# Key latent first, and the memory output weights in two strips, in a three-block transformer kernel

## The reference, cut to what matters

```
x = x + 0.5 * swiglu(rms_norm(x, ffn1_norm), ffn1_w_in, ffn1_w_out)
z = rms_norm(x, mix_norm) @ w_mix_in
z_mla, z_swa, z_na = split(z)                 # cq (256) | ckv (128) | rotary key (32) = z_mla
  q  = rms_norm(cq, g)  @ w_uq                # 8 heads of 96
  kv = rms_norm(ckv, g) @ w_ukv               # 8 heads of 64 (key) + 64 (value)
x = x + concat(norm(mla), norm(swa), norm(na)) @ w_mix_out
x = x + mem_xattn(rms_norm(x, g), mem, ...)   # o (512 x 256) @ w_o (256 x 1024)
x = x + 0.5 * swiglu(rms_norm(x, ffn2_norm), ffn2_w_in, ffn2_w_out)
x = rms_norm(x, block_norm)
```

## Time and profile before

| | |
|---|---|
| time, median of 3 runs | 3268.42 us (3264.87 to 3268.74) |
| time of the profiled execution | 3268.41 us |
| its span, first to last instruction | 3266.6 us |
| PE busy | 3000.9 us, 92% of the span |
| DVE, ACT, POOL busy | 1460.0, 1086.3, 251.1 us (45%, 33%, 8%) |
| mean granted PE clock | 0.960 of full |
| the 16 DMA engines, busy | 21.4% for the main queue's packets |

### The profile page before, as it was taken

How to read it: one execution, slowest core, us unless ns; L and a number is a source line. 1 busy time by engine, 2 the same in 40 slices (tenths; PEclk the granted TensorE clock), 3 DMA queues, 4 the chain that set the end, 5 groups by cost and what they waited for, 6 DMA issues and landing times. The chain is left out here.

```text
span 3266.6 us, 37293 instructions
## 1 busy us (share of the span) xinstructions
PE 3000.9 (92%) x13472; PEld 2357.7 (72%) x13472; DVE 1460.0 (45%) x2022; ACT 1086.3 (33%) x1770; POOL 251.1 (8%) x184
## 2 busy tenths in 40 slices
PE   8878998999799998998889999699998998899997
PEld 5567676678588887577668888488885677668885
DVE  5653255643444423555344442444424554354432
ACT  4412233343233312555242321232213654333221
POOL 0000000000200012000220002200021001120011
PEclk9989899999899999999999999799998999999998
DMA  3100220113223323010212232132322110122231
GB/s 121 45 20 7 75 77 33 58 46 96 97 96 96 101 96 109 16 56 20 70 60 96 96 102 78 60 96 97 105 83 91 33 52 27 45 91 96 96 104 69
DMA packets 69081, 238.07 MB, mean 73 GB/s; under 512 B 10353, under 2 KB 14449, under 8 KB 68209
## 3 DMA queue, kind: packets, MB, share of 16 engines
q1 hardware_dynamic: 66960, 227.87, 21.4%
q10 hardware_dynamic: 2016, 8.84, 0.7%
HBM read 234.58 MB, written 2.10 MB: 72 GB/s over the span
## 5 line engine op out<-in xcount | busy, mean ns | idle before, releaser
L368 PE MATMUL bank<-L_h_hi,L_w_hi 128*128 128x512 f32 x1808 | 720.9, 399 | 72.3 <-DVE L_h_lo L477 39.0
L369 PE MATMUL bank<-L_h_lo,L_w_hi 128*128 128x512 f32 x1808 | 712.9, 394 | 0.0
L370 PE MATMUL bank<-L_h_hi,L_weight_ring_low 128*128 128x512 f32 x1808 | 712.9, 394 | 0.0
L356 ACT CAST L_w_hi<-L_weight_ring 128x1024 fp32r<-128x1024 f32 (+2 forms) x292 | 326.3, 1118 | 952.0 <-PE bank L370 946.7
L362 DVE TENSOR_TENSOR L_weight_ring_low<-L_weight_ring,L_w_hi 128x1024 fp32r<-128x1024 f32 (+2 forms) x292 | 401.4, 1375 | 358.9 <-ACT L_w_hi L356 358.9
L368 PEld LDWEIGHTS bank<-L_h_hi,L_w_hi 128*128 128x128 f32 x1808 | 345.2, 191 | 162.0 <-issue 56.8
L370 PEld LDWEIGHTS bank<-L_h_hi,L_weight_ring_low 128*128 128x128 f32 x1808 | 344.9, 191 | 72.8
L369 PEld LDWEIGHTS bank<-L_h_lo,L_w_hi 128*128 128x128 f32 x1808 | 345.4, 191 | 71.6 <-issue 1.0
L368 PE MATMUL bank<-L_act_hi,L_w_hi 128*128 128x512 f32 x704 | 273.9, 389 | 0.0
L369 PE MATMUL bank<-L_act_lo,L_w_hi 128*128 128x512 f32 x704 | 273.9, 389 | 0.0
L370 PE MATMUL bank<-L_act_hi,L_weight_ring_low 128*128 128x512 f32 x704 | 273.9, 389 | 0.0
(11 more groups left out here) (283 smaller groups left out, 3878.9 us busy)
## 6 DMA issues: line engine op xcount, KB each, us to landing
L_weight_ring<-ffn_in SPq DMA_DIRECT2D x176, 512.0 KB, 3.4
L_weight_ring<-ffn_out SPq DMA_DIRECT2D x64, 704.0 KB, 4.1
B_weight_ring<-w_sqk SPq DMA_DIRECT2D x24, 512.0 KB, 3.4
B_weight_ring<-w_dn SPq DMA_DIRECT2D x16, 512.0 KB, 3.5
B_weight_ring<-w_gate SPq DMA_DIRECT2D x16, 512.0 KB, 3.4
L_weight_ring<-w_sna_qk SPq DMA_DIRECT2D x16, 512.0 KB, 3.4
L_weight_ring<-w_mix_out SPq DMA_DIRECT2D x16, 512.0 KB, 3.5
B_weight_ring<-w_sv SPq DMA_DIRECT2D x12, 512.0 KB, 3.5
```

The lines of the kernel that those rows point to most:

```text
L356: e.copy(hv.high(at)[:, 0:width], sh.ring[:, at % RING, 0:width]).then_inc(hv.w_hi_done, 1)
L368: e.matmul(out, a_hi, b_hi, start=start, stop=False)
L369: e.matmul(out, a_hi, b_lo, start=False, stop=False)
L370: return e.matmul(out, a_lo, b_hi, start=False, stop=stop)
```

## The change

It has two parts.

**Latents.** The three latent strips are loaded in the order ckv, cq, cq, so that ckv lies in bank 4 and cq in banks 5 and 6. The sum of ckv's squares (into bank 0) moves ahead of the last strip, krope; the two for cq stay behind it (bank 1). ACT makes ckv's 1/rms before it squares the rotary key, and DVE writes the normalised ckv before it touches the rotary key. PE then makes v_mla after waiting only for ckv (lat_done 1), in banks 0, 2, 3 and 4, and waits for the other latents behind v_mla. As bank 0 is also the first job's, that job gets a wait for ACT's first copy of v_mla.

**Memory output.** The host lays w_mem_o out as two strips of 128 x 1024, each for four tiles of x. PE runs the eight tiles in straight code, signalling mem_mm after the tiles that do not end a strip. Since six strips fewer pass the ring, the next block's first two strips lie in it before the memory attention ends. ACT splits the first ahead of its copies of the transposed result and the second behind them; DVE splits both ahead of its first addition to x.

```diff
             mix_jobs.append(dict(parts=[[(0, cq[:, 0, :]), (P, cq[:, 1, :])]], rows=(0, P), width=T,
                                  ones=(ones, QK2), scale=1.0 / QK2, gain=qg[:, 0:1], rope="own", cos_sin=cs2,
-                                 dest=(qk[:, tile, :], QK2), split=h == MLA_HEADS - 1))
+                                 dest=(qk[:, tile, :], QK2), split=h == MLA_HEADS - 1,
+                                 **({"needs": (v_done, TT + 1)} if h == 0 else {})))
...
-                for i in range(3):
+                for i in (2, 0, 1):
                     at = load_strip(e, seen, sh, at, A["w_latent"][layer, i])
...
-                at = resid_sp(e, seen, sh, at, lambda n, part: A["w_mem_o"][layer, n], 1)
+                for i in range(2):
+                    at = load_strip(e, seen, sh, at, A["w_mem_o"][layer, i])
...
+                def lat_sum(k):
+                    e.wait_ge(sh.squared, seen.ready(sh.squared))
+                    e.matmul(banks[0 if k < 1 else 1][:, :], ones, sh.sq[:, k % 2, :], start=(k != 2),
+                             stop=(k != 1)).then_inc(sh.sum_mm, 1)
...
-                e.wait_ge(v_done, seen.ready(v_done, TT))
-                for k in range(3):
-                    e.wait_ge(sh.squared, seen.ready(sh.squared))
-                    e.matmul(banks[0 if k < 2 else 1][:, :], ones, sh.sq[:, k % 2, :], start=(k != 1),
-                             stop=(k != 0)).then_inc(sh.sum_mm, 1)
-                e.wait_ge(lat_done, seen.ready(lat_done, 4))
+                    if i == 2:
+                        e.wait_ge(v_done, seen.ready(v_done, TT))
+                        lat_sum(0)
+                lat_sum(1)
+                lat_sum(2)
+                e.wait_ge(lat_done, 1)
                 w = strip_here(e, seen, sh, at)
                 at += 1
                 for t in range(TT):
-                    mm = e.matmul(banks[4 + t][:, :], ckv[:, 0, t * P:(t + 1) * P], w[:, 0:512], start=True,
+                    mm = e.matmul(banks[(0, 2, 3, 4)[t]][:, :], ckv[:, 0, t * P:(t + 1) * P], w[:, 0:512], start=True,
                                   stop=True)
                 mm.then_inc(sh.strip_done, 1)
                 seen.ready(v_done, TT)
+                e.wait_ge(lat_done, seen.ready(lat_done, 4))
...
-                at = resid_pe(e, seen, sh, at, o_memT, 1, 2)
+                for n in range(KT):
+                    e.wait_ge(sh.x_done, seen.free(sh.x_done))
+                    if n % 4 == 0:
+                        w = strip_here(e, seen, sh, at)
+                        at += 1
+                    for k in range(2):
+                        c = (n % 4 * 2 + k) * P
+                        mm = e.matmul(banks[4 + n % 2][:, :], w[:, c:c + P], o_memT[:, k, :], start=(k == 0),
+                                      stop=(k == 1))
+                    mm.then_inc(sh.strip_done if n % 4 == 3 else mem_mm, 1)
```

More of the change, by code:

```diff
@@ L1398, in _, with latent_rstd @@
                     e.copy(grid_tiles(v_rows[1 + f]), grid_rows(banks[1 + f][:, :])).then_inc(vt_done, 1)
+                def latent_rstd(n, bank, dst):
+                    e.wait_ge(sh.sum_mm, seen.ready(sh.sum_mm, n))
+                    e.activation(dst[:, :], banks[bank][:, :], ACT.Ln, scale=1.0 / (n * P),
+                                 bias=EPS).then_inc(sh.ln_done, 1)
+                    e.wait_ge(sh.ln_done, seen.ready(sh.ln_done))
+                    e.activation(dst[:, :], dst[:, :], ACT.Exp, scale=-0.5).then_inc(sh.rstd_done, 1)
                 for k in range(3):
@@ L1408, in _ @@
                             e.copy(v_sna[:, t, :], banks[t][:, 0:384]).then_inc(v_done, 1)
+                latent_rstd(1, 0, lat_rstd)
                 e.wait_ge(sh.strip_done, seen.ready(sh.strip_done))
                 e.activation(jb.sq[NOPE:QK2, 1, :], banks[7][NOPE:QK2, :], ACT.Square).then_inc(kr_sq, 1)
-                for i, (n, bank, dst) in enumerate(((2, 0, sh.rstd), (1, 1, lat_rstd))):
-                    e.wait_ge(sh.sum_mm, seen.ready(sh.sum_mm, n))
-                    e.activation(dst[:, :], banks[bank][:, :], ACT.Ln, scale=1.0 / (n * P),
-                                 bias=EPS).then_inc(sh.ln_done, 1)
-                    e.wait_ge(sh.ln_done, seen.ready(sh.ln_done))
-                    e.activation(dst[:, :], dst[:, :], ACT.Exp, scale=-0.5).then_inc(sh.rstd_done, 1)
+                latent_rstd(2, 1, sh.rstd)
                 e.wait_ge(sh.strip_done, seen.ready(sh.strip_done))
                 for t in range(TT):
-                    e.copy(v_mla[:, t, :], banks[4 + t][:, :]).then_inc(v_done, 1)
+                    e.copy(v_mla[:, t, :], banks[(0, 2, 3, 4)[t]][:, :]).then_inc(v_done, 1)
                 def group_norms():
@@ L1513, in _ @@
                 seen.ready(sh.strip_done, 9)
+                e.wait_ge(sh.rstd_done, seen.ready(sh.rstd_done))
+                e.scalar_tensor_tensor(out=ckv[:, 0, :],
+                                       in0=banks[4][:, :], scalar=g("ckv"), in1=lat_rstd[:, :],
+                                       op0=ALU.mult, op1=ALU.mult).then_inc(lat_done, 1)
                 e.wait_ge(kr_sq, 1)
@@ L1526, in _ @@
                 for k in range(2):
-                    e.scalar_tensor_tensor(out=cq[:, k, :], in0=banks[4 + k][:, :], scalar=g("cq")[:, k:k + 1],
+                    e.scalar_tensor_tensor(out=cq[:, k, :], in0=banks[5 + k][:, :], scalar=g("cq")[:, k:k + 1],
                                            in1=sh.rstd[:, :], op0=ALU.mult, op1=ALU.mult).then_inc(lat_done, 1)
-                e.wait_ge(sh.rstd_done, seen.ready(sh.rstd_done))
-                e.scalar_tensor_tensor(out=ckv[:, 0, :],
-                                       in0=banks[6][:, :], scalar=g("ckv"), in1=lat_rstd[:, :],
-                                       op0=ALU.mult, op1=ALU.mult).then_inc(lat_done, 1)
                 def scale_groups():
@@ L1586, in _ @@
                            unit=attn_dve_steps(e, seen, sh, at_, mem_units, stores("mem", o_mem, 2)))
+                for i in range(2):
+                    split_strip_dve(e, seen, sh, hv, ffn2_at + i, W_IN)
                 for n in range(KT):
-                    e.wait_ge(sh.strip_done, seen.ready(sh.strip_done))
+                    if n % 4 == 3:
+                        e.wait_ge(sh.strip_done, seen.ready(sh.strip_done))
+                    else:
+                        e.wait_ge(mem_mm, seen.ready(mem_mm))
                     x = xT[:, n, :]
@@ L2597, in layout2 @@
     out["w_mem_v"] = np.swapaxes(kv[..., 256:].reshape(L, 2, 4, P, 256), 2, 3).reshape(L, 2, P, 1024)
-    out["w_mem_o"] = rows_first(a["mem_w_o_2"], P)
+    out["w_mem_o"] = np.swapaxes(rows_first(a["mem_w_o_2"], P).reshape(L, 2, 4, P, 256), 2, 3).reshape(L, 2, P, 1024)
     col = lambda x: np.swapaxes(x.reshape(L, -1, P), 1, 2)
```

13 lines of the change are left out of this document (6 added, 7 removed).

## The result

| | before | after |
|---|---|---|
| median of 4 runs each | 3268.41 us (3264.87 to 3268.74) | 3237.48 us (3234.05 to 3240.96) |
| ratio | | 0.9916, 95% interval 0.9892 to 0.994 |
| span of the profiled execution | 3266.6 us | 3232.3 us |
| mean granted PE clock | 0.960 | 0.966 |

The kernel became 30.9 us faster, where 24.0 were forecast.

What follows compares the result with a forecast made beforehand. PE, busy 92% of the span, was taken as the bound, so only its idle or half-clock time could be saved. 12.5 (latents) + 11.5 (memory output) = 24.0 us off 3268.4 gave 3244.4 us, range 3240 to 3257.

Steps and rivals of the forecast that it cites:

- The latents' term: Latents: v_mla from E+2.7, first job E+6.95 (E: first sum of squares' start, before the change); 6.8 plus 5.7, 12.5 us.
- the lower bound: Latents: at least 7.8 us gained, if v_mla kept its old 6.50 and 5.40 us.
- upper bound: Latents: at most 13.8 us gained, if job 0 followed v_mla at once.
- The memory output's term: Next feed-forward block: strip 0 follows the output passes without a gap, 5.7 us sooner per layer, 11.5 us together.
- The covers: Memory output: all four moved splits fall in ACT's and DVE's waiting time, 0.8 us to spare for the last.
- Output weights at nothing: Memory output: the 32 passes keep their pace, mean 0.50 us; fewer loads and loop instructions gain nothing.
- Sum: Whole kernel: 12.5+11.5 = 24.0 us gained, from 3268.4 to 3244.4 us.
- the rest of the span should keep its lengths: Sign to check: outside the latents and the memory output, nothing in the span changes length.
- the old low bound: Lower end of the forecast range, 3240 us: 13.8+11.5 gained, with a microsecond or two for a vanishing slow start.
- Rival 1: At v_mla and the two first strips the clock falls all the same, taking 8.4 us: 3252.8 us, chance 0.12.
- Rivals 2 and 3: 2: latents' or memory half of the gain lost, 3256.9 or 3255.9 us, chance 0.09; 3: nothing gained, 3268, chance 0.04.
- Rival 4: Woven stretch: its new start lets the clock swing to 1.2 GHz; 64 us of it gives 3276 us, chance 0.03.

Runs made afterwards that it cites:

- bank7: Changed kernel with value products in banks 2, 3, 4 and 7, the fourth waiting for the first key copy: 3238.99 us.
- b_only: Kernel before with only the memory output's part, the two strips and early splits: 3255.27 us.
- b_split_late: Changed kernel with ACT's and DVE's splits of the next two strips put back where they stood before the change: 3254.84 us.
- a_only: Kernel before with only the new order of the latents: 3256.18 us.
- fill: Changed kernel with unread products of a constant added in three idle places of PE in each layer's memory stage: 3227.68 us.
- again: Changed kernel, unaltered, measured a second time: 3241.21 us.
- again2: Changed kernel, unaltered, measured once more: 3241.94 us.
- a_wait: Changed kernel with PE waiting for all four latent tiles before the value products, instead of the first alone: 3248.54 us.
- both: Changed kernel with the bank move of `bank7` and the constant products of `fill` together: 3228.37 us.
- before_fill: Kernel before with unread constant matmuls added in both idle stretches of each layer, order of work unchanged: 3256.05 us.

## Why the prediction was right, and where it was off

*The latents' term, 12.5 us.* Right. Forecast and found in layer 1: value products at E+2.7 and E+2.60; first job at E+6.95 and E+7.08; gain 6.8 and 6.7. Layer 2: 5.7 and 5.6, the old 12.66 less the new 7.08. Together 12.3 (in layer 2 the rotary key's strip of after ended at 2479.59 and the job began at 2486.67). The value products kept neither their 6.50 nor their 5.40 us, so the lower bound did not come; nor did job 0 follow at once, so neither did the upper one. The key latent was ready 4.4 us early and not 2: by the prediction's own rows krope's 5.44 and the two sums' 1.8 cover a chain of 2.0, so the 2 was too low, on the safe side. `bank7` shows that this upper bound can be reached, by another bank.

*The memory output's term, 11.5 us.* Right: 5.86 in each layer in the table, 11.7 together. Of it 5.6 is what the prediction named, the gap and the slow first strip; the other 0.3 lies ahead of the output passes, whose wait behind the transposes became 0.67 us instead of 0.95. `b_only` and `b_split_late` have it and `a_only` not, so it comes with the straight code or the two strips, which the prediction had set at nothing. The covers held, with more to spare than I said: 1.67 us instead of 0.8 ahead of the first addition, because DVE's low halves took 1.23 us there and not the 2.28 that I had set. `b_split_late` shows that the mechanism is the one named, the splits' place in the queues, at its full price.

*Output weights at nothing.* Right: 16.06 us against 15.96 in layer 1, 16.02 against 15.87 in layer 2. But the price of the slow start was in these rows all the time: `fill` makes the same passes in 14.00.

*Sum.* 12.3 + 11.7 = 24.0, the forecast; that it fits to the tenth is luck, since the two terms were 0.2 and 0.3 too large and 0.6 us, the 0.3 in each layer ahead of the output passes, was not counted. The step that was off is "the rest of the span should keep its lengths". In `again` three pieces of unchanged code became shorter: 1.0 us between the layers (6.57 less 5.6), 1.3 in the second woven stretch and 0.8 in the tail, 3.1 together, which with the 24.1 of the two places makes its 27.2. All three can be read from rows, and in all three it is the clock. The first and the last are a matmul of the norm behind a wait for POOL. Timelines of PE, two rows of before, then two of `again`:

```profile
2051.36 2.07 PE L221 MATMUL bank<-L_squares_sum,shared_consts 128*128 128x512 f32 x2 [3.24 <-POOL L_squares_sum L215]
3246.15 2.07 PE L221 MATMUL bank<-L_squares_sum,shared_consts 128*128 128x512 f32 x2 [3.24 <-POOL L_squares_sum L215]
...
2038.72 1.13 PE L221 MATMUL bank<-L_squares_sum,shared_consts 128*128 128x512 f32 x2 [3.24 <-POOL L_squares_sum L215]
3219.80 1.12 PE L221 MATMUL bank<-L_squares_sum,shared_consts 128*128 128x512 f32 x2 [3.24 <-POOL L_squares_sum L215]
```

The wait is the same, and the granted clock is 0.50 in before (window 3246.00:3248.00) and 1.00 in `again` (window 3219.80:3220.90). The 1.3 us are the fall of the clock behind the first wait of 1.90 us in the woven stretch, which before has in layer 2 and `again` has not (last section). I set all this at nothing and gave it no width; an execution of the same kernel moves up to 7 us there. A lower end of 3237, the old low bound less these 3, would have held the first median too; and the recorded terms, 13.8+11.5 and a microsecond or two, give 3241 to 3242 as low end and not the 3240 written. Is the shorter tail a part of the change? After, `again`, `again2`, `b_only`, `a_wait`, `bank7` and `fill` have the fast matmul there, before, `a_only`, `b_split_late` and `both` the slow one. `both` carries the whole change, so the change does not bring it by itself, and `before_fill` (1.35 us) has most of it without the change. What decides the clock in unchanged code stays open.

*Rival 1*, the clock falling all the same, did not come at the two places. Elsewhere it lives: see the last section. *Rivals 2 and 3* fell with `a_only` and `b_only`, each of which gives its own half. *Rival 4*: in no kernel did a woven piece become longer than before by more than 0.70 us; the new start of it kept its 0.94.

## What to carry to other kernels

Idle time on the engine that bounds is paid twice when a lower clock follows it, so the price of a gap is its length plus half of what runs at half clock behind it. It does not follow every time: behind the same short wait it came in one execution and not in the next (last section). Here that second part was some 8 of 24 us, and cheap constant products in gaps that could not be closed brought 13.5 us on top. When an operand is made of several tiles by several engines, look for the first consumer that needs only one of them, and wait for that one. And when a block starts late, look at what stands ahead of its preparation in the preparing engine's order before the transfers: there the early load alone was worth nothing.

## What the runs showed of the hardware

*The same wait is followed by the lower clock in one place and not in another.* Some 15.3 us behind the start of the first job, PE waits 1.90 us for ACT's first probabilities, in each of these kernels. The windows of the next 4 us, layers 1 and 2 of `again`, then layer 1 of `bank7` and of `b_split_late`:

```profile
1325.82:1329.82 4.00, 3.67 (x12) 2.32 (x13) 0.75 (x2) 2.52 (x8) 0.00 (x0) 0.66 0.00 0
2508.89:2512.89 4.00, 3.67 (x20) 2.43 (x20) 1.42 (x3) 2.79 (x8) 0.00 (x0) 1.00 0.00 0
```

```profile
1323.98:1327.98 4.00, 3.65 (x20) 2.41 (x20) 1.42 (x3) 2.81 (x8) 0.00 (x0) 1.00 0.00 0
...
1328.32:1332.32 4.00, 3.67 (x20) 2.43 (x20) 1.42 (x3) 2.78 (x8) 0.00 (x0) 1.00 0.00 0
```

Over all twelve kernels, two layers each, the clock fell behind this wait in 12 of 24 cases. With the 0.88 us of idle time ahead of the first job (after, `again`, `again2`, `a_only`, `b_split_late`, `fill`) it fell in 7 of 12; with no idle time ahead of the first job or of the value products (`bank7`, `both`) in none of 4; with 0.72 us (`a_wait`) in none of 2; and with idle time ahead of the value products alone (before, `b_only`, `before_fill`) in 5 of 6. That an earlier short wait can cost more than itself some 15 us later is therefore a guess that these counts allow and do not show: `b_split_late` has the latents of `again` to the row, 0.88 us included, and the clock stayed up in both of its layers. The norm's matmul tells the same: behind waits of 3.24 and 3.84 us it took 2.07 or 2.08 us in 12 of 48 cases and 1.12 to 1.35 in the others. The Trainium skill ("TensorE: Matmul & The Clock Gate", under "A second HAM failure mode") says that idle pauses between groups of matmuls can make the clock swing; the trace agrees here, while at the two places of the change nothing of it was left to see. This was the mechanism of rival 1, at another place.

*DVE's low half of a strip has two durations.* It took 1.22 to 1.23 us where POOL was idle (1647.62 and 1651.33 after) and 2.28 to 2.30 in before and in `b_split_late` beside POOL's squares, which then took 2.02 us instead of 1.04. At 1673.08 after it took 1.23 with POOL at work, and POOL's sum beside it 2.36 instead of 1.29:

```profile
1673.09 2.36 POOL L215 TENSOR_TENSOR L_squares_sum<-L_squares_sum,L_tile_squares 128x512 f32<-128x512 f32 x1
```

So where the two run beside each other one of them or both take some 1 us longer, and which of them pays differs. Splitting early took the halves out of each other's way, which the prediction had not counted; it had spare time there and gained nothing by it.
